# High-half products of a pair of weight pieces first, low-half products last, in a mixture-of-experts stage

## The chip, the core and the metric

The kernel runs on one core of one Trainium2 chip. Its metric is device time in microseconds for one execution. Each run gives one such time; a profiled execution gives a trace beside it.

## The reference, cut to what matters

Two blocks of two layers each run over 256 tokens of width 1024. The change touches only the feed-forward part of the first block's second layer, a mixture of eight experts of which each token uses two:

```
logits = x @ w_router + b_router
top_vals, top_idx = top_k(logits, 2);  top_w = softmax(top_vals)
combine = sum(one_hot(top_idx, 8) * top_w[..., None], axis=-2)
for e in range(8):
    out += combine[..., e:e+1] * ((silu(x @ w_gate[e]) * (x @ w_up[e])) @ w_down[e])
```

`w_gate` and `w_up` are 1024x3584 for each expert and `w_down` is 3584x1024, all in float32.

## The kernel before

**Three products for one.** TensorE multiplies fp32r numbers, which keep fewer bits than float32. Each float32 operand is therefore held as two fp32r tiles: a high half (the value rounded) and a low half (the value less the high half). A product is the sum of three: high activations by high weights, high activations by low weights, low activations by high weights. `Tensor.mm3` issues them in this order for one slice of 128 rows. The activations are the operand that is loaded (LDWEIGHTS), the weights are the one that streams by, 512 columns at a time, into one bank of PSUM.

**How weights come.** The class `Weights` plans every weight of the program in order. A load brings 1 MB (128 x 2048 floats) from memory into one of five raw buffers `RG`, on SyncE's queue. In the experts' stage a load is cut into a pair of pieces of 1024 columns. ScalarE copies each piece into the high tile (`his`, two ACTIVATEs of 128x1024 per pair). VectorE then writes the low tile of the whole pair with one subtraction of 128x2048 (`los`, the case `both`). The three pairs of tiles are a ring: two are in `WH` (high) and `WL` (low), the third is in `MW`, which holds both halves, so rows that name `MW` are a pair of either half. Three counters order it. `P.hi` rises with each piece that ScalarE has copied. `P.lo` rises with each pair that VectorE has finished, and SyncE refills a raw buffer once it has risen. `P.used` rises when TensorE has finished a piece, and ScalarE waits for it before it overwrites that piece (`p.prev`).

**The stage.** For each expert, 128 gathered tokens are the rows, and the 3584 hidden columns are done in 7 steps of 512. The program numbers the 56 steps j, with `todo[j] = (e, n)`. A step on TensorE is, in this order:

1. G: the gate product, two pairs (24 matmuls), the first of them in `MW`.
2. U: the up product, two pairs (24 matmuls), the first in `WH`/`WL`, the second in `MW`.
3. the extras: at n = 3 the gather of the next expert's tokens (32 small matmuls), at n = 4 two transposes for putting tokens back, at n = 1 the scatter of the last expert's result (8 matmuls, the second half of which waits for VectorE's additions).
4. D: the down product of the step before, two pairs (24 matmuls), into two banks.
5. four transposes of the activated hidden block, once VectorE has multiplied it.

ScalarE's queue for step j is: the high halves of U, silu of G, the high halves of D, at n = 3 the gather's modulation (8 small ACTIVATEs and two copies), the high halves of the next G, at n = 0 the copies of the finished expert's result, and the high half of the transposed block. VectorE's queue is: the low halves of U and D, the multiplication, at n = 1 the scatter's additions, the low halves of the next G, then the low half of the gathered tokens (n = 3) or of the result (n = 0), and the low half of the transposed block. Each engine works through its queue in program order.

The lines that the change touches are `up` and `down` inside `pe_moe`. Both wait for `P.lo` of a pair before any product of it. In the rows below, L205 is the matmul helper, L213 the transpose helper, L197 `act` on ScalarE, L167 `tt` on VectorE (`ATR` is the transposed block, `HTR` the gathered tokens, `DER` the result), L171 `ts` and L175 `stt`.

Of the kernel before, what the change touches and what calls it, by code (L numbers as in the profile page):

```python
# [372 lines left out]
def build(nc, w):  # L373
    ctx = ExitStack()
    with ctx:
# [43 lines left out]
        PS = ctx.enter_context(nc.psum_tensor("PS", [128, 8, 512], F32))  # L419
# [19 lines left out]
        def tok(t):  # L439
            return slice(t * 128, (t + 1) * 128)  # L440
# [1493 lines left out]
        EAT = [ATR[:, z * 1024:(z + 1) * 1024].rearrange("p (u k n) -> p u k n", u=2, k=4) for z in range(2)]  # L1934
        HE = [HTR[:, z, :].rearrange("p (u k n) -> p u k n", u=2, k=8) for z in range(2)]
# [7 lines left out]
        def pe_moe(pe, P, s_pe, s_v, s_a):  # L1943
            def gather(e):
                u = e % 2
                pe.wait_ge(s_v, e, "pp")
                for g in range(2):
                    if e:
                        pe.wait_ge(s_a, e - 1, f"gm{g}")
                        if e > 1:  # L1950
                            pe.wait_ge(s_v, e - 2, f"acc1{g}")
                        if g == 0:
                            pe.wait_ge(s_a, e - 1, "pt")
                    for k in range(4):
                        for t in range(2):
                            x = pe.mm(PS[:, 2 + g, k * 128:(k + 1) * 128], X[:, t, (g * 4 + k) * 128:(g * 4 + k + 1) * 128],
                                      PP[:, u, t], t == 0, t == 1)
                    x.then_inc(s_pe, f"ga{g}")

            def put_back(e):  # L1960
                u = e % 2
                pe.wait_ge(s_a, e, "gm0")
                for t in range(2):
                    x = pe.tr(PS[:, 2, tok(t)], PP[:, u, t], IDN)
                x.then_inc(s_pe, "pb")

            def up(parts, b, u):
                for p in parts:
                    pe.wait_ge(P.lo, p.los)
                    for k in range(p.kk):  # L1970
                        kk = p.k0 + k
                        x = pe.mm3(PS[:, b, :], HE[0][:, u, kk, :], HE[1][:, u, kk, :], p.h3[:, k, :], p.l3[:, k, :], kk == 0,
                                   kk == 7)
                    x.then_inc(P.used)

            def scatter(e):
                u = e % 2
                pe.wait_ge(s_a, e, "pt")
                for t in range(2):
                    for h in range(2):  # L1980
                        c = slice(h * 512, (h + 1) * 512)
                        pe.wait_ge(s_v, e, f"de{h}")
                        if t:
                            pe.wait_ge(s_v, e, f"acc0{h}")
                        elif e:
                            pe.wait_ge(s_v, e - 1, f"acc1{h}")
                        pe.mm(PS[:, 2 + h, :], PT[:, u, tok(t)], DE[0][:, c], True, False)
                        pe.mm(PS[:, 2 + h, :], PT[:, u, tok(t)], DE[1][:, c], False, True).then_inc(s_pe, f"sc{t}{h}")

            def down(j):  # L1990
                e, n = todo[j]
                for p in P.of["moe_down", e, n]:
                    pe.wait_ge(P.lo, p.los)
                    pe.wait_ge(s_v, j, "at")
                    if n == 0 and e:
                        for h in range(2):
                            pe.wait_ge(s_v, e - 1, f"de{h}")
                    i = p.k0
                    for h in range(2):
                        c = slice(h * 512, (h + 1) * 512)  # L2000
                        x = pe.mm3(PS[:, h, :], EAT[0][:, j % 2, i, :], EAT[1][:, j % 2, i, :], p.h3[:, 0, c], p.l3[:, 0, c],
                                   n == 0 and i == 0, n == 6 and i == 3)
                    x.then_inc(P.used)

            gather(0)
            put_back(0)
            for j, (e, n) in enumerate(todo):
                u = j % 2
                if n == 0:
                    for g in range(2):  # L2010
                        pe.wait_ge(s_v, e, f"he{g}")
                if j >= 2:
                    pe.wait_ge(s_v, j - 2, "at")
                up(P.of["moe_gate", e, n], 4 + 2 * u, e % 2)
                if j >= 2:
                    pe.wait_ge(s_v, j - 2, "ac")
                up(P.of["moe_up", e, n], 5 + 2 * u, e % 2)
                if n == 3 and e + 1 < NE:
                    gather(e + 1)
                if n == 4 and e + 1 < NE:  # L2020
                    put_back(e + 1)
                if n == 1 and e:
                    scatter(e - 1)
                if j:
                    down(j - 1)
                pe.wait_ge(s_v, j, "ac")
                for i in range(4):
                    x = pe.tr(PS[:, 4 + 2 * u, i * 128:(i + 1) * 128], EAC[:, u, i * 128:(i + 1) * 128], IDN)
                x.then_inc(s_pe, "at")
            down(len(todo) - 1)  # L2030
            scatter(NE - 1)

# [1285 lines left out]
```

## Time and profile before

| what | value |
|---|---|
| median of three runs | 2967.05 us (2965.32 to 2967.56) |
| span of the profiled execution | 2961.7 us |
| TensorE busy (modelled ends) | 2550.9 us, 86% |
| weight loads of TensorE | 2001.1 us, 68% |
| VectorE busy | 2062.3 us, 70% |
| ScalarE busy | 1557.5 us, 53% |
| 16 DMA engines in the experts' stage | 89% |

The span is measured from the first to the last instruction of one profiled execution; no separate time of that execution is listed, so 5.35 us is what lies between its span and the median of the runs. Times in the rows are microseconds from the start of that span. The experts' stage reaches from about 905 to 1988 us. TensorE's matmul ends are modelled, so its waits are read from its weight loads (PEld), each of which stands just before its matmul.

### The profile page before, as it was taken

What the parts mean: (1) busy time and instruction counts of PE and PEld (TensorE: products, weight loads), DVE (VectorE), ACT (ScalarE), POOL (GpSimd) and SP (SyncE); (2) the same over time, 40 slices, a digit from 0 to 9 for tenths busy, and PEclk for the clock granted to TensorE, in tenths of its full rate; (3) what the DMA queues carried; (4) which work ended last, traced back from release to release, by engine and by line L of the source; (5) the groups of instructions that cost most, each with busy time, mean ns of one, the idle gap of its engine ahead of it and who ended that gap; (6) DMA issues with size and microseconds to landing.
All of it is one profiled execution on the core that took longest, in us unless ns stands there. A gap on an engine that the chain in (4) does not pass through costs nothing.

```text
span 2961.7 us, 31514 instructions
## 1 busy us (share of the span) xinstructions
PE 2550.9 (86%) x11727; PEld 2001.1 (68%) x11727; DVE 2062.3 (70%) x2214; ACT 1557.5 (53%) x1920; POOL 24.0 (1%) x33
## 2 busy tenths in 40 slices
PE   6977789977967999999999999976777998886898
PEld 2736677856556777777777777765556786655787
DVE  6687786755666888787878888875665554575454
ACT  1222434442156778787777777764534544544443
POOL 0000000000100000000000000000000000000000
PEclk8997999986978999999999999998877999977899
DMA  7450367732335898898989899984112454303352
GB/s 252 160 164 29 106 214 263 270 120 71 100 114 200 323 332 324 300 361 291 362 302 353 330 333 329 335 295 136 44 43 100 157 185 156 109 15 114 104 188 93
DMA packets 274306, 598.03 MB, mean 202 GB/s; under 512 B 28705, under 2 KB 35167, under 8 KB 272993
## 3 DMA queue, kind: packets, MB, share of 16 engines
q1 hardware_dynamic: 252144, 580.30, 55.2%
q10 hardware_dynamic: 22002, 15.66, 2.0%
q8 instruction: 93, 1.52, 0.2%
q14 instruction: 67, 0.55, 0.1%
HBM read 594.86 MB, written 1.06 MB: 201 GB/s over the span
## 4 chain that ended last, share of the span: by engine, by line
PE 61%; DVE 24%; ACT 10%; issue 2%; ACTq 2%; DMA 1%; DVEq 0%; POOL 0%; POOLq 0%; PEldq 0%
PE PS L205 58%; DVE WL L167 8%; ACT WH L197 3%; ACT AR L197 2%; PE PS L213 2%; DVE MW L167 2%; DVE AR L167 2%; ACTq L146 2%; DVE WF L167 1%; DVE MOD L167 1%; ACT MW L197 1%; ACT L197 1%; DVE HF L167 1%; ACT WF L197 1%; DVE HTR L167 1%
## 5 line engine op out<-in xcount | busy, mean ns | idle before, releaser
L167 DVE TENSOR_TENSOR WL<-RG,WH 128x1024 fp32r<-128x1024 f32 (+1 forms) x558 | 919.4, 1648 | 447.4 <-ACT WH L197 422.8
L197 ACT ACTIVATE WH<-RG 128x1024 fp32r<-128x1024 f32 x782 | 827.3, 1058 | 597.4 <-PE PS L205 527.2
L205 PE MATMUL PS<-WH,HTR 128*128 128x512 f32 (+3 forms) x2920 | 926.0, 393 | 66.8 <-DVE HTR L167 23.4
L205 PEld LDWEIGHTS PS<-WH,HTR 128*128 128x128 f32 x2920 | 558.0, 194 | 201.0 <-DVE WL L167 39.8
L205 PE MATMUL PS<-WL,HTR 128*128 128x512 f32 (+3 forms) x1460 | 568.9, 390 | 0.0
L205 PE MATMUL PS<-WH,ATR 128*128 128x512 f32 x1624 | 523.6, 396 | 16.4 <-DVE WL L167 9.1
L205 PEld LDWEIGHTS PS<-WH,ATR 128*128 128x128 f32 x1624 | 310.3, 191 | 84.7 <-DVE WL L167 18.3
L205 PE MATMUL PS<-MW,HTR 128*128 128x512 f32 x1332 | 331.1, 398 | 18.2 <-DVE MW L167 18.2
L205 PE MATMUL PS<-WL,ATR 128*128 128x512 f32 x812 | 320.4, 395 | 0.0
L205 PEld LDWEIGHTS PS<-WL,HTR 128*128 128x128 f32 x1460 | 283.2, 194 | 52.4
L167 DVE TENSOR_TENSOR MW<-RG,MW 128x2048 fp32r<-128x2048 f32 x112 | 256.7, 2292 | 63.3 <-ACT MW L197 52.6
L205 PEld LDWEIGHTS PS<-MW,HTR 128*128 128x128 f32 x1332 | 249.0, 190 | 70.6 <-DVE MW L167 20.1
L197 ACT ACTIVATE MW<-RG 128x1024 fp32r<-128x1024 f32 x224 | 237.9, 1062 | 24.7 <-PE PS L205 2.1
L205 PEld LDWEIGHTS PS<-WL,ATR 128*128 128x128 f32 x812 | 155.2, 191 | 31.9
L213 PE MATMUL PS<-KC,AR 128*128 128x128 f32 (+2 forms) x716 | 115.8, 300 | 59.5 <-DVE AR L167 34.6
L213 PEld LDWEIGHTS PS<-KC,AR 128*128 128x128 f32 (+2 forms) x716 | 94.6, 155 | 85.7 <-DVE AR L167 41.0
L197 ACT ACTIVATE AR<-PS 128x512 f32<-128x512 f32 (+3 forms) x112 | 63.7, 569 | 107.0 <-PE PS L205 59.1
L197 ACT ACTIVATE AR<-PS,SMALL 128x128 f32<-128x128 f32 (+3 forms) x146 | 77.6, 531 | 73.3 <-PE PS L205 65.4
L197 ACT ACTIVATE ATR<-PS 128x512 fp32r<-128x512 f32 x102 | 61.2, 600 | 80.5 <-PE PS L213 75.5
L205 PE MATMUL PS<-RG,CZ 128*4 128x512 f32 x192 | 92.6, 636 | 10.5 <-DMA RG<-in_mod_w 9.8
L213 PE MATMUL PS<-KC,X 128*128 128x128 f32 x160 | 31.8, 377 | 80.3 <-ACTq L155 30.4
L213 PEld LDWEIGHTS PS<-KC,X 128*128 128x128 f32 x160 | 27.9, 200 | 84.6 <-DVEq L155 36.6
(224 smaller groups left out, 2057.5 us busy)
## 6 DMA issues: line engine op xcount, KB each, us to landing
RG<-in_moe_w_gate SPq DMA_DIRECT2D x112, 1024.0 KB, 5.4
RG<-in_moe_w_up SPq DMA_DIRECT2D x112, 1024.0 KB, 5.8
RG<-in_moe_w_down SPq DMA_DIRECT2D x112, 1024.0 KB, 6.0
RG<-in_w_ff SPq DMA_DIRECT2D x64, 1024.0 KB, 5.2
RG<-in_mod_w SPq DMA_DIRECT2D x48, 1024.0 KB, 5.2
RG<-in_w_in SPq DMA_DIRECT2D x36, 1024.0 KB, 5.2
RG<-in_w_out SPq DMA_DIRECT2D x16, 1024.0 KB, 5.1
RG<-in_ffn_w_gate SPq DMA_DIRECT2D x14, 1024.0 KB, 5.2
```

The lines of the kernel that those rows point to most:

```text
L146: return Ins(self.e.dma_start(dst, src, **kw) if self.e is not None else None, self)
L167: return self.did(lambda: self.e.tensor_tensor(o, a, b, op))
L197: return self.did(lambda: self.e.activation(o, a, f, bias=bias, scale=scale))
L205: return self.did(lambda: self.e.matmul(o, l, r, start=start, stop=stop))
L213: return self.did(lambda: self.e.transpose(o, a, perm))
```

## The change

TensorE takes the two pieces of a pair together. For each piece it waits for ScalarE's high half of that piece and issues the two products that need only high weights (high activations, then low activations). Then it waits for the pair's low half and issues the third product for both pieces, each followed by its `P.used`. In `down` the waits for the activated block and for the last result's tiles stand once, ahead of all pieces. The number of matmuls, their shapes and their banks stay, and so do the queues of all other engines.

```diff
             def up(parts, b, u):
-                for p in parts:
-                    pe.wait_ge(P.lo, p.los)
-                    for k in range(p.kk):
-                        kk = p.k0 + k
-                        x = pe.mm3(PS[:, b, :], HE[0][:, u, kk, :], HE[1][:, u, kk, :], p.h3[:, k, :], p.l3[:, k, :], kk == 0,
-                                   kk == 7)
-                    x.then_inc(P.used)
+                for pair in (parts[0:2], parts[2:4]):
+                    for p in pair:
+                        pe.wait_ge(P.hi, p.i + 1)
+                        for k in range(p.kk):
+                            kk = p.k0 + k
+                            pe.mm(PS[:, b, :], HE[0][:, u, kk, :], p.h3[:, k, :], kk == 0, False)
+                            pe.mm(PS[:, b, :], HE[1][:, u, kk, :], p.h3[:, k, :], False, False)
+                    for p in pair:
+                        pe.wait_ge(P.lo, p.los)
+                        for k in range(p.kk):
+                            kk = p.k0 + k
+                            x = pe.mm(PS[:, b, :], HE[0][:, u, kk, :], p.l3[:, k, :], False, kk == 7)
+                        x.then_inc(P.used)
 
             def down(j):
                 e, n = todo[j]
-                for p in P.of["moe_down", e, n]:
-                    pe.wait_ge(P.lo, p.los)
-                    pe.wait_ge(s_v, j, "at")
-                    if n == 0 and e:
+                parts = P.of["moe_down", e, n]
+                pe.wait_ge(s_v, j, "at")
+                if n == 0 and e:
+                    for h in range(2):
+                        pe.wait_ge(s_v, e - 1, f"de{h}")
+                for pair in (parts[0:2], parts[2:4]):
+                    for p in pair:
+                        pe.wait_ge(P.hi, p.i + 1)
                         for h in range(2):
-                            pe.wait_ge(s_v, e - 1, f"de{h}")
-                    i = p.k0
-                    for h in range(2):
-                        c = slice(h * 512, (h + 1) * 512)
-                        x = pe.mm3(PS[:, h, :], EAT[0][:, j % 2, i, :], EAT[1][:, j % 2, i, :], p.h3[:, 0, c], p.l3[:, 0, c],
-                                   n == 0 and i == 0, n == 6 and i == 3)
-                    x.then_inc(P.used)
+                            c = slice(h * 512, (h + 1) * 512)
+                            pe.mm(PS[:, h, :], EAT[0][:, j % 2, p.k0, :], p.h3[:, 0, c], n == 0 and p.k0 == 0, False)
+                            pe.mm(PS[:, h, :], EAT[1][:, j % 2, p.k0, :], p.h3[:, 0, c], False, False)
+                    for p in pair:
+                        pe.wait_ge(P.lo, p.los)
+                        for h in range(2):
+                            c = slice(h * 512, (h + 1) * 512)
+                            x = pe.mm(PS[:, h, :], EAT[0][:, j % 2, p.k0, :], p.l3[:, 0, c], False, n == 6 and p.k0 == 3)
+                        x.then_inc(P.used)
```

## Rows read from the trace of the kernel before

**Rows 1.** The page's first line.

```profile
span 2961.7 us, 31514 instructions
```

**Rows 2.** Windows of stage and steady steps: busy us (instructions) by engine, clock, DMA share, GB/s.

```profile
905.00:1988.00 1083.00, 1019.30 (x4574) 823.09 (x4572) 897.82 (x528) 830.33 (x886) 0.00 (x0) 0.99 0.89 325
1545.00:1596.00 51.00, 51.00 (x230) 41.51 (x229) 45.26 (x25) 41.85 (x42) 0.00 (x0) 1.00 1.03 379
1566.00:1600.00 34.00, 34.00 (x153) 27.66 (x152) 30.49 (x17) 28.43 (x30) 0.00 (x0) 1.00 1.04 393
```

**Rows 3.** Waits of TensorE's weight loads, 905 to 1978: us, times, longest.

```profile
PEld PS L205 <- DVE WL L167: 40.2, 56, 2.8
PEld PS L205 <- DVE AR L175: 23.2, 14, 3.1
PEld PS L205 <- DVE MW L167: 20.1, 8, 2.6
```

**Rows 4.** Timeline of weight loads: start, us, work, count, [idle before it <- releaser].

```profile
926.94 2.59 PEld L205 LDWEIGHTS PS<-MW,HTR 128*128 128x128 f32 x12 [1.98 <-DVE MW L167]
...
1550.88 0.19 PEld L205 LDWEIGHTS PS<-WH,HTR 128*128 128x128 f32 x1 [0.30 <-DVE WL L167]
...
1567.88 0.19 PEld L205 LDWEIGHTS PS<-WH,HTR 128*128 128x128 f32 x1 [0.30 <-DVE WL L167]
...
1945.55 0.19 PEld L205 LDWEIGHTS PS<-WH,HTR 128*128 128x128 f32 x1 [0.30 <-DVE WL L167]
```

**Rows 5.** Timelines of ScalarE and VectorE, from 1545 us.

```profile
1545.57 0.60 ACT L197 ACTIVATE ATR<-PS 128x512 fp32r<-128x512 f32 x1 [0.89 <-PE PS L213]
1546.28 2.21 ACT L197 ACTIVATE WH<-RG 128x1024 fp32r<-128x1024 f32 x2
...
1548.53 2.29 DVE L167 TENSOR_TENSOR WL<-RG,WH 128x2048 fp32r<-128x2048 f32 x1 [0.66 <-ACT WH L197]
```

**Rows 6.** Timelines of weight loads, ScalarE and VectorE around one gather.

```profile
1523.28 0.58 PEld L213 LDWEIGHTS PS<-KC,AR 128*128 128x128 f32 x4
1526.46 2.61 PEld L205 LDWEIGHTS PS<-MW,HTR 128*128 128x128 f32 x12 [2.59 <-DVE MW L167]
...
1533.64 0.19 PEld L205 LDWEIGHTS PS<-WH,HTR 128*128 128x128 f32 x1 [1.85 <-DVE WL L167]
...
1516.46 3.96 ACT L197 ACTIVATE AR<-PS,SMALL 128x128 f32<-128x128 f32 x8 [2.45 <-PE PS L205]
...
1521.87 2.21 ACT L197 ACTIVATE MW<-RG 128x1024 fp32r<-128x1024 f32 x2
...
1524.11 2.29 DVE L167 TENSOR_TENSOR MW<-RG,MW 128x2048 fp32r<-128x2048 f32 x1 [6.88 <-ACT MW L197]
...
1528.90 1.49 DVE L167 TENSOR_TENSOR HTR<-AR,HTR 128x512 fp32r<-128x512 f32 x2
...
1531.29 2.30 DVE L167 TENSOR_TENSOR WL<-RG,WH 128x2048 fp32r<-128x2048 f32 x1
```

**Rows 7.** Around scatters: two weight-load rows, then three pieces of the chain.

```profile
1062.20 0.19 PEld L205 LDWEIGHTS PS<-WH,HTR 128*128 128x128 f32 x1 [1.47 <-DVE WL L167]
...
1871.55 0.19 PEld L205 LDWEIGHTS PS<-WH,HTR 128*128 128x128 f32 x1 [1.45 <-DVE WL L167]
...
1462.58 0.61 ACT DER L197
...
1479.69 6.19 PE PS L205 x26
...
1207.99 7.81 PE PS L205 x26
```

**Rows 8.** Waits of ScalarE, 905 to 1976: us, times, longest.

```profile
ACT WH L197 <- PE PS L205: 49.6, 31, 6.4
...
ACT MW L197 <- PE PS L205: 2.1, 6, 0.5
ACT WH L197 <- DMA RG<-in_moe_w_gate: 1.6, 2, 1.2
```

## The prediction

> **What bounds the kernel now.** I read the busy time by windows first: it says which engine is close to full in the experts' stage. Then I read TensorE's waits in that stage, and last the timelines of the three engines at each kind of wait, because only there can one see what is late next. All sums are made against the profiled span of 2961.7 us [rows 1]; the median of the runs is 5.35 us more, and I add that at the end.
>
> The stage takes 1083 us, 37% of the span. TensorE's matmuls are shown busy for 1019 us of it, VectorE for 898, ScalarE for 830, the DMA engines for 89% [rows 2]. So TensorE sets the pace, but the others follow closely, and a wait that is removed can come back at another place.
>
> TensorE waits for low halves 64 times, for 40.2 + 20.1 = 60.3 us, and for the scatter's additions 14 times, for 23.2 us [rows 3]. The change can only touch the 60.3 us. A product row of 12 loads takes 2.61 us, so one product of 512 columns costs about 0.22 us [rows 6], and the eight products with high weights of a pair take 8 x 0.22 = 1.8 us. The change lets TensorE run them before the low half is there: each wait shrinks by up to 1.8 us, if the high half is there and if the time is not lost again further on. A gap of some 0.04 us stands before every load anyway, and I take it off each wait.
>
> **The change by places.** I sorted the 64 waits by where they stand.
>
> *Forty-one short waits in ordinary steps.* The first is 1.98 us, the last 0.30 us [rows 4]; most are 0.25 to 0.55 us, and they add up to 19.9 us. The pattern is in one step: ScalarE's copy of the transposed block waits for TensorE's transposes and starts at 1545.57, the high half of U's first pair takes 1546.28 to 1548.49, VectorE's low half 1548.53 to 1550.82 [rows 5], and TensorE starts U at 1550.88 [rows 4]. The high half is there about 2 us before G ends, and the low half will be wanted 1.8 us after U starts, so it is in time with 1.5 us to spare. Nothing else stands behind: a step then takes 17.00 - 0.26 = 16.74 us, while VectorE's own work in a step is six subtractions and two small ones, 6 x 2.4 + 2 x 0.8 = 16.0 us with gaps. Six of the longer ones are 0.9 to 1.2 us (in the first four experts, where VectorE has an operation more between its low halves), so the 1.8 us cover them; the first, 1.98 us, is covered but for 0.1 us. The working: 19.9 - 41 x 0.04 = 18.3 us gained.
>
> *Seven gathers, with two waits each.* Here ScalarE is late: it does the eight modulations from 1516.46 and two copies, and only then the high half of G's first pair, 1521.87 to 1524.08. TensorE is ready at about 1523.9 and waits 2.59 us, until VectorE is through at 1526.40; then it waits 1.85 us more before U, until VectorE's low half of that pair, 1531.29 to 1533.59, is done [rows 6]. After the change it starts G at once, since both high pieces are there in time, and wants G's first low half at 1523.9 + 1.8 = 1525.7, for which it waits 0.7 us. G's two pairs of 2.7 us then end at 1530.0, U's low half is wanted at 1531.8, and that comes no earlier than before: VectorE is busy without a gap from 1524.11 over the tokens' low halves at 1528.90 to 1533.59 [rows 6]. That is the binding event in both kernels. Before, twelve products of the pair follow it; after, four. So the gain is 8 x 0.22 = 1.76 us, not the 4.4 us of the two waits: 7 x 1.75 = 12.3 us. A wait of 1533.6 - 1531.8 = 1.8 us stays inside U's first pair. In three of the seven gathers the second wait is short and the pair before it runs at a lower clock; from the start of G to the start of U it is 7.18 us in each of the seven, so the argument is the same.
>
> *Seven waits just ahead of a scatter.* The first is 1.47 us, the last 1.45 us [rows 7]; together 11.0 us. I count nothing for them. From the copy of the finished expert's result at 1462.58, ScalarE works without a gap (result, transposed block, high halves of U, silu, high halves of D), then VectorE takes over with the low halves of D, the multiplication and the additions, and TensorE goes on at 1479.69 [rows 7]. This path of 17.1 us does not run through TensorE's U. TensorE will reach the scatter 1.5 us earlier and wait there 1.5 us longer: the waits for additions should grow from 23.2 us to about 34 us.
>
> *The end of the stage.* The last wait for a low half (2.8 us, the longest in [rows 3]) also covers the transposed block, which VectorE makes after the low halves; `down` waits for it first in either kernel. It and the 0.30 us ahead of it give nothing.
>
> *What is added.* TensorE has three waits for a pair instead of one, 672 more in 336 pairs. I take them at nothing: while TensorE is busy its waits are met long before, and 51 us of ordinary steps show it busy for 51.00 us with a wait at every second piece [rows 2]. From the other side, if one cost as much as the gap that stands before each load anyway, 0.04 us, they would take 27 us; see the rivals. The first piece of a pair is given back after product 10 instead of 6, 0.9 us later. ScalarE waits for TensorE's pieces 31 times in `WH` [rows 8]. Where it does, the pair's high half is finished 0.65 us later, because the second piece is given back at the same time as before; TensorE has 1.8 us more patience for the low half, so this is hidden. At the other places ScalarE comes later than the release anyway. The moved waits in `down` stand where the first piece's stood, and nothing new is queued behind them.
>
> *The clock.* After a scatter's wait TensorE sometimes runs at 1.2 instead of 2.4 GHz for a while: the same 26 products take 7.81 us after one scatter and 6.19 us after another [rows 7]. This is so in five of the seven. With a wait that is 1.5 us longer I expect it in all seven: 2 x 1.6 = 3 us lost.
>
> Sum: 18.3 + 12.3 - 3.0 = 27.6 us. 2961.7 - 27.6 = 2934.1 us of span, and with the 5.35 us 2939.5; I say 2940 us.
>
> **The rivals.**
>
> *The transfers set the pace (12 in 100).* A step reads six loads of 1.049 MB, 6.29 MB. At 16.74 us a step that is 376 GB/s. Ordinary steps show 379 GB/s over 51 us with a DMA share of 1.03, and 393 GB/s over 34 us [rows 2], the extra being a catch-up; ScalarE waited for a transfer twice, 1.6 us in all [rows 8]. So there are 4% to spare. If they are not usable, because transfers land later when they overlap more, the ordinary steps stay at 17.0 us: some 33 of the short waits, 33 x 0.26 = 8.6 us, come back as waits for ScalarE's high halves. Time: 2948 us. The Trainium skill (HBM Reference, Specifications) puts the effective rate of a core at about 358 GB/s; by it a step could not take less than 17.6 us and the change would bring nothing. This trace disagrees: 393 GB/s here, with one core at work, and I keep the measured rate.
>
> *The clock falls more often (10 in 100).* The clock fell in three of the seven gathers too, where it was hidden behind U's low half. After the change the waits there are 0.7 and 1.8 us instead of 2.6 and 1.9, which speaks against it. If it fell in all seven behind the binding event, it would cost 7 x 1.6 = 11 us: 2951 us. The Trainium skill (TensorE: Matmul & The Clock Gate, Part 1) says the array is slow by default and activity frees it, which agrees with the two durations of 26 products.
>
> *More comes back (7 in 100).* If VectorE's chain behind a gather itself moves forward, the 26.3 us of the two waits are all gained instead of 12.3: 2926 us. Against it stands VectorE without a gap there.
>
> *The added waits cost (5 in 100).* At 0.04 us each, 27 us, they would eat the gain: 2967 us, no change. For it: after a wait a load starts 0.04 us later. Against: nothing is seen at the waits that are already met.
>
> *Slower, by the later release (4 in 100).* At 37 places (31 in `WH`, six in `MW`) ScalarE stands waiting for TensorE [rows 8]. If there the loop ScalarE, VectorE, TensorE is closed, each costs up to 0.9 us, 33 us; it decides from 0.82 us a place on (30.6 / 37), where it equals the gain. With the clock's 3 us it makes 2973 us. Against it: the low half may now be 1.8 us late at no cost, twice the delay.
>
> **How the numbers follow.** The forecast has 62 in 100. The range of 2928 to 2956 us takes in the transfers and the clock and reaches almost to the greater gain; that one, the added waits and the slower case are left out, 16 in 100, and some 4 in 100 for mixtures beyond it. What a measurement of this kernel can tell from no change is 0.2%, 6 us. Faster by more than that: 62 + 12 + 10 + 7 = 91 in 100, less one for a mixture of the losses: 90. Within 0.2%: 5. Slower: 5.
>
> **What would show it.** In the trace after: waits for low halves fall from 60 us to about 20 us (seven of 1.8 and seven of 0.7 us after gathers, 2.8 at the end), now standing at loads of the last four products; waits for additions rise to about 34 us; ordinary steps take 16.7 us instead of 17.0; an expert takes about 3.2 us less, the first four somewhat more; the stages before 905 us and after the last expert are unchanged. Waits for high halves longer than 0.1 us in ordinary steps would mean that transfers or releases bind, and small gaps at the start of each piece that the added waits cost.

## The result, and the profile after

The changed kernel takes 2946.05 us (median of four runs, 2943.81 to 2952.73) against 2967.31 us. The ratio of the runs is 0.9933, with a 95% interval of 0.9921 to 0.9945: 16 to 23 us faster. I had forecast 2940 us. The run with the profile took 2947.36 us. Its page begins as follows (the first two lines, and the chain by line):

```profile
span 2945.6 us, 31514 instructions
...
PE 2539.9 (86%) x11727; PEld 2008.4 (68%) x11727; DVE 2062.1 (70%) x2214; ACT 1557.1 (53%) x1920; POOL 23.9 (1%) x33
...
PE PS L205 62%; DVE WL L167 6%; PE PS L213 3%; ACT AR L197 2%; DVE MW L167 2%; DVE AR L167 2%; ACTq L146 2%; DVE WF L167 1%; DVE MOD L167 1%; ACT WH L197 1%; DVE HF L167 1%; ACT L197 1%; DVE HTR L167 1%; ACT WF L197 1%; DVE SMALL L178 1%
```

The same work is done, and the other engines are as busy as before. In this execution the experts' stage begins 4.3 us later than in the one of before (its first four transposes load at 928.87 us against 924.54 us), for reasons ahead of the change. So I compare the stage by itself, from those transposes to the last ones of the 56 steps: 1048.84 us before, 1029.27 us after, 19.6 us less.

The waits of TensorE's weight loads from 905 to 1978 us (us, times, longest), to be held against [rows 3]:

```profile
PEld PS L205 <- DVE AR L175: 34.3, 16, 4.5
PEld PS L205 <- DVE WL L167: 15.5, 10, 2.0
PEld PS L205 <- DVE MW L167: 6.8, 8, 0.9
```

The waits for low halves fell from 60.3 us in 64 places to 22.3 us in 18. The last of the 64, 2.8 us at the stage's end, is not among the 18: it is now put down to the transposed block, with 3.0 us. The stage now ends earlier, so this window takes in two waits for additions at its end that the window of [rows 3] leaves out. Without these two the waits for the scatter's additions are 33.2 us in 14 places: they rose by 10.0 us from 23.2.

The timeline of one gather, first the weight loads, then VectorE (start, us, work, count, idle before). It answers to [rows 6]:

```profile
1511.98 0.58 PEld L213 LDWEIGHTS PS<-KC,AR 128*128 128x128 f32 x4
1512.53 1.69 PEld L205 LDWEIGHTS PS<-MW,HTR 128*128 128x128 f32 x8
1515.14 0.76 PEld L205 LDWEIGHTS PS<-MW,HTR 128*128 128x128 f32 x4 [0.92 <-DVE MW L167]
1515.95 1.78 PEld L205 LDWEIGHTS PS<-WH,HTR 128*128 128x128 f32 x8
1517.77 0.87 PEld L205 LDWEIGHTS PS<-WL,HTR 128*128 128x128 f32 x4
1518.68 1.77 PEld L205 LDWEIGHTS PS<-WH,HTR 128*128 128x128 f32 x8
1522.32 0.76 PEld L205 LDWEIGHTS PS<-WL,HTR 128*128 128x128 f32 x4 [1.87 <-DVE WL L167]
...
1512.80 2.29 DVE L167 TENSOR_TENSOR MW<-RG,MW 128x2048 fp32r<-128x2048 f32 x1 [6.48 <-ACT MW L197]
1515.19 2.29 DVE L167 TENSOR_TENSOR WL<-RG,WH 128x2048 fp32r<-128x2048 f32 x1
1517.59 1.49 DVE L167 TENSOR_TENSOR HTR<-AR,HTR 128x512 fp32r<-128x512 f32 x2
1519.18 0.69 DVE L167 TENSOR_TENSOR ATR<-PS,ATR 128x512 fp32r<-128x512 f32 x1
1519.98 2.29 DVE L167 TENSOR_TENSOR WL<-RG,WH 128x2048 fp32r<-128x2048 f32 x1
```

Here one sees the change: eight loads, then four. After the transposes TensorE starts G's first pair at once. It waits 0.92 us for the first low half, goes through G's second pair, and waits 1.87 us inside U's first pair. VectorE has no gap from 1512.80 on, and its low half of that pair ends at 1522.27.

The timeline of the weight loads at one scatter, to be held against [rows 7]:

```profile
1457.55 2.68 PEld L205 LDWEIGHTS PS<-MW,HTR 128*128 128x128 f32 x12
1460.27 0.87 PEld L205 LDWEIGHTS PS<-DER,PTR 128*128 128x128 f32 x4
1465.69 0.50 PEld L205 LDWEIGHTS PS<-DER,PTR 128*128 128x128 f32 x2 [4.55 <-DVE AR L175]
1466.54 0.50 PEld L205 LDWEIGHTS PS<-DER,PTR 128*128 128x128 f32 x2 [0.35 <-DVE AR L175]
1467.14 3.32 PEld L205 LDWEIGHTS PS<-WH,ATR 128*128 128x128 f32 x8
1470.55 1.49 PEld L205 LDWEIGHTS PS<-WL,ATR 128*128 128x128 f32 x4
1472.08 1.77 PEld L205 LDWEIGHTS PS<-WH,ATR 128*128 128x128 f32 x8
1473.90 0.87 PEld L205 LDWEIGHTS PS<-WL,ATR 128*128 128x128 f32 x4
```

No low half is waited for, and TensorE is at the scatter early; then it stands for 4.55 us. Behind that wait eight loads take 3.32 us, and 1.77 us five microseconds later: the clock has fallen. The windows of the granted clock behind this scatter, and one behind the same scatter in the kernel before, which is one of the two of its seven behind which the clock had not fallen (busy us of PE, PEld, DVE, ACT, POOL with counts, granted clock, DMA share, GB/s):

```profile
1466.50:1469.90 3.40, 3.40 (x9) 2.68 (x9) 2.74 (x3) 0.00 (x0) 0.00 (x0) 0.50 0.75 297
1469.90:1473.30 3.40, 3.40 (x12) 2.68 (x12) 1.05 (x1) 1.16 (x2) 0.00 (x0) 0.71 0.39 76
1473.30:1476.70 3.40, 3.40 (x19) 2.82 (x18) 2.30 (x2) 1.88 (x3) 0.00 (x0) 1.00 0.57 235
```

```profile
1479.70:1483.10 3.40, 3.40 (x15) 2.83 (x16) 3.15 (x3) 1.06 (x1) 0.00 (x0) 1.00 0.63 251
```

After: 0.50 (1.2 GHz), then 0.71 in a window that holds both levels, then 1.00. Before, with a wait of 3.08 us: 1.00 (2.4 GHz).

The 56 sets of transposes bound 55 steps, each from one set to the next. Taking them apart shows where the 19.6 us come from (sums in us):

| steps | before | after | difference |
|---|---|---|---|
| seven behind a gather | 149.9 | 137.2 | -12.8 |
| seven with a scatter | 169.2 | 178.3 | +9.1 |
| the other 41 | 729.7 | 713.9 | -15.9 |

An ordinary step went from 17.00 to 16.80 us. A step with a scatter went from 23.2 to 24.9 us to 24.1 to 26.8 us.

### The profile page after: what moved, and what is told of

The parts are those of the page before. It is cut to its first block, busy times and chain, and to the rows that moved or that the text cites. A ratio compares the mean times of both kernels' runs of the same rounds, so it can differ in the third digit from the quotient of the medians.

```text
span 2945.6 us, 31514 instructions
## 1 busy us (share of the span) xinstructions
PE 2539.9 (86%) x11727; PEld 2008.4 (68%) x11727; DVE 2062.1 (70%) x2214; ACT 1557.1 (53%) x1920; POOL 23.9 (1%) x33
## 4 chain that ended last, share of the span: by engine, by line
PE 65%; DVE 22%; ACT 7%; issue 2%; ACTq 2%; DMA 2%; DVEq 0%; POOL 0%; POOLq 0%; PEldq 0%
PE PS L205 62%; DVE WL L167 6%; PE PS L213 3%; ACT AR L197 2%; DVE MW L167 2%; DVE AR L167 2%; ACTq L146 2%; DVE WF L167 1%; DVE MOD L167 1%; ACT WH L197 1%; DVE HF L167 1%; ACT L197 1%; DVE HTR L167 1%; ACT WF L197 1%; DVE SMALL L178 1%
## 5 line engine op out<-in xcount | busy, mean ns | idle before, releaser
L205 PE MATMUL PS<-WH,HTR 128*128 128x512 f32 (+3 forms) x2920 | 850.4, 391 | 47.5 <-DVE HTR L167 23.4
L205 PE MATMUL PS<-WL,HTR 128*128 128x512 f32 (+3 forms) x1460 | 513.9, 390 | 11.6 <-DVE WL L167 11.6
L205 PE MATMUL PS<-WH,ATR 128*128 128x512 f32 x1624 | 465.4, 400 | 16.2 <-DVE WL L167 8.9
L205 PE MATMUL PS<-WL,ATR 128*128 128x512 f32 x812 | 265.3, 393 | 0.0
L197 ACT ACTIVATE MW<-RG 128x1024 fp32r<-128x1024 f32 x224 | 237.9, 1062 | 24.2 <-DMA RG<-in_moe_w_gate 1.5
```

The costliest lines, as they stand in the source:

```text
L197: return self.did(lambda: self.e.activation(o, a, f, bias=bias, scale=scale))
L205: return self.did(lambda: self.e.matmul(o, l, r, start=start, stop=stop))
```

## The experiments

Twelve kernels ran, in three rounds of four and each round on another chip, always beside the kernel before (2966.2, 2968.3 and 2968.1 us). The times in this table are medians in us. The ratio is to the kernel before on the same chip, so it is the better measure between rounds.

| run | edit | us | ratio (95%) |
|---|---|---|---|
| after_again | none | 2945.0 | 0.9926 (0.9905 to 0.9947) |
| up_only | new order in gate and up alone | 2952.0 | 0.9958 (0.9945 to 0.9971) |
| down_only | new order in down alone | 2965.4 | 0.9989 (0.9980 to 0.9997) |
| after_busy | changed kernel, products in the scatter's wait | 2934.0 | 0.9895 (0.9875 to 0.9914) |
| before_busy | kernel before, products in the scatter's wait | 2960.6 | 0.9977 (0.9966 to 0.9989) |
| up_busy | gate and up alone, products in the wait | 2945.6 | 0.9927 (0.9915 to 0.9939) |
| piecewise | low half waited for in each piece | 2952.2 | 0.9953 (0.9940 to 0.9966) |
| more_waits | 2016 waits added that are already met | 2947.6 | 0.9925 (0.9912 to 0.9939) |
| rows_moved | two rows loaded at a gather | 2945.2 | 0.9923 (0.9910 to 0.9937) |
| split_scatter | changed kernel, scatter's second half behind down | 2916.4 | 0.9819 (0.9803 to 0.9835) |
| before_split | kernel before, the same split | 2975.4 | 1.0023 (1.0012 to 1.0033) |
| split_rows | split_scatter and rows_moved | 2912.6 | 0.9821 (0.9806 to 0.9837) |

**The changed kernel again.**

> The changed kernel once more, beside the others on the same chip. Both theories: some 2946 us, 0.993 of the kernel before. The theory that the clock takes back a part of the gain expects the seven steps with a scatter to be 9 us longer in sum than before again (between 6 and 12, since the clock's falls vary), and every other step to be shorter.

It took 2945.0 us, and its seven scatter steps are again the long ones, 24.1 to 26.1 us. The granted clock fell behind each.

**Is it the clock? Products in the wait.** The scatter gets N products that nobody reads, between its two halves. N is 17 in the changed kernel, 10 in the kernel before, 15 with gate and up alone:

```diff
                 for t in range(2):
+                    if t and j is not None:
+                        pe.wait_ge(s_v, j - 1, "at")
+                        for i in range(N):
+                            pe.mm(PS[:, 6 - 2 * (j % 2), :], PT[:, u, tok(0)], DE[0][:, 0:512], True, True)
                     for h in range(2):
```

> The changed kernel with 17 products of 512 columns more in each of the seven scatters, between its two halves, where TensorE otherwise waits 4.2 to 4.5 us for VectorE's additions; they write a bank that nobody reads afterwards, so nothing else is computed. Theory (the clock falls during that wait and TensorE runs slowly behind it): the granted clock stays at 1.00 in all seven, the steps with a scatter shrink from some 25.5 us to some 23 us, and the kernel takes 2946 - 14 = 2932 us, at least under 2938 us. Rival (those steps are longer for another reason, as a late transfer or a late high half): no gain, 2946 us or some more.

> The kernel before with 10 such products in the same place, where it waits 2.7 to 3.1 us. Theory: five of its seven scatters ran slowly behind the wait, 1.5 us each, so it gains 7 us: 2960 us. Beside the run with the 17 products it then shows the change without the clock: 28 us apart. Rival: 2967 us, and 21 us apart.

Both came out as the theory said: 2934.0 and 2960.6 us. The timeline and a window of the changed kernel with the products:

```profile
1454.62 4.72 PEld L205 LDWEIGHTS PS<-DER,PTR 128*128 128x128 f32 x21
1460.04 0.30 PEld L205 LDWEIGHTS PS<-DER,PTR 128*128 128x128 f32 x2 [0.70 <-DVE AR L175]
1460.90 0.30 PEld L205 LDWEIGHTS PS<-DER,PTR 128*128 128x128 f32 x2 [0.56 <-DVE AR L175]
1461.24 1.80 PEld L205 LDWEIGHTS PS<-WH,ATR 128*128 128x128 f32 x8
```

```profile
1440.00:1475.00 35.00, 34.60 (x156) 28.03 (x155) 30.23 (x21) 24.28 (x27) 0.00 (x0) 1.00 0.90 311
```

TensorE waits as long for the additions, since it only fills the time, and it comes back at full clock: the eight loads take 1.80 us instead of 3.32. Work that computes nothing gains 11 us on the changed kernel and 5.6 us on the one before. Taken apart by steps, the scatter steps are 163.4 us with the products against 178.3 without, and in the kernel before 161.8 against 169.2. So the clock's falls cost 14.8 us after and 7.4 us before. All other steps together are unchanged within 0.1 us.

**Which part gives the gain?**

> Only the gate and up products take the new order, the down products keep the old one. Theory (no wait for a low half that mattered stood ahead of a down product): the same time as the changed kernel within 3 us, 2946 us. Rival (the new order in the down products gives a part of the gain, since their pairs come right behind VectorE's low halves): half of the gain is missing, 2955 us.

> Only the down products take the new order, gate and up keep the old one. In the kernel before no wait for a low half stood at a down pair except the last; with gate and up alone changed, waits of 0.24 and 0.88 us appeared there. Theory (the new order of the down pairs only covers waits that the earlier arrival brings): no gain by itself, 2967 us within 3 us. Rival (its own part is what the run with gate and up alone lacked, 7 us): 2960 us.

> Gate and up in the new order, down in the old, with 15 products more in each scatter to hold the clock. Theory (without the clock's falls the down part of the change is worth 10 us, since the step with gate and up alone waits 0.24 us at an ordinary down pair and 0.88 us behind a gather): 2944 us, 10 us above the changed kernel with its 17 products and 16 below the kernel before with its 10. Rival (the down part is worth 6 us as without the extra products): 2940 us.

The theory for the first was wrong: gate and up alone take 2952.0 us, 7 us more than the whole change. Weight loads of that kernel behind a gather:

```profile
1526.21 0.77 PEld L205 LDWEIGHTS PS<-WL,HTR 128*128 128x128 f32 x4 [1.87 <-DVE WL L167]
...
1531.01 0.19 PEld L205 LDWEIGHTS PS<-WH,ATR 128*128 128x128 f32 x1 [0.88 <-DVE WL L167]
```

TensorE, now early, meets the next pair's low half too soon: 0.88 us here, and 0.24 us at the down pair of each ordinary step, which takes 16.91 us instead of 16.80. In the kernel before, no down pair waited, save the last. Down alone takes 2965.4 us, 2.7 us less than before with an interval that ends at 0.9997, so by itself it is worth next to nothing. With the clock held, the down part on top of gate and up is worth 2945.6 - 2934.0 = 11.6 us. These two ran on different chips, but the stages of their traces, 1026.1 and 1014.4 us, differ by as much. I had expected 10. The new order in gate and up uncovers waits that the new order in down must then cover.

**How far ahead must TensorE be able to go?** Here each piece waits for its own low half, after four products instead of eight, and is released as early as before:

```diff
-                for pair in (parts[0:2], parts[2:4]):
-                    for p in pair:
+                for p in parts:
                         pe.wait_ge(P.hi, p.i + 1)
...
-                    for p in pair:
-                        pe.wait_ge(P.lo, p.los)
+                    pe.wait_ge(P.lo, p.los)
```

> Each piece by itself: wait for its high half, four products with high weights, wait for the pair's low half, two products, release. TensorE can then go only 4 x 0.22 = 0.9 us ahead of a low half instead of 1.8 us, and each piece is released as early as in the kernel before. Theory (what counts is how many products stand ahead of the wait for the low half): seven gathers lose 0.9 us each and the ordinary waits of 0.3 us stay covered, but the waits of 1 to 1.2 us show again: some 8 us slower than the changed kernel without the clock's part; with longer steps ahead of the scatters its waits there are shorter, so 2950 us, between 2946 and 2956. Rival (the early release matters): 2940 us or less.

2952.2 us, as the theory had it. Weight loads behind the same gather:

```profile
1516.75 1.69 PEld L205 LDWEIGHTS PS<-MW,HTR 128*128 128x128 f32 x8 [1.85 <-DVE MW L167]
...
1523.93 0.30 PEld L205 LDWEIGHTS PS<-WL,HTR 128*128 128x128 f32 x2 [1.87 <-DVE WL L167]
```

The first wait is 0.93 us longer than the 0.92 us of the changed kernel: four products. A step behind a gather takes 20.5 us instead of 19.6, and the steps of the first experts in which VectorE has an operation more take 17.1 to 17.3 us instead of 16.79. Ordinary steps stay at 16.80 us: four products ahead are enough for their wait of 0.3 us. The early release of the first piece brought nothing that could be seen.

**Do the added waits cost?** Three waits are repeated behind each wait for a low half, that is six for a pair:

```diff
                         pe.wait_ge(P.lo, p.los)
+                        pe.again(P.lo, p.los)
+                        pe.again(P.lo, p.los)
+                        pe.again(P.lo, p.los)
```

> The changed kernel with six more waits for each pair on TensorE (three behind each wait for the low half), all of them already met when they are reached. Theory (a wait that is met is hidden behind the matmuls under way): 2946 us, ordinary steps stay at 16.80 us. Rival (each costs 0.04 us): six pairs a step, 36 waits, 1.4 us a step, 56 steps: 80 us slower.

2947.6 us, and the ordinary steps take 16.79 or 16.80 us as before. The stage took 1029.59 us against 1029.27. The steps behind a gather are 0.2 us longer each: their first wait for a low half is 1.10 us instead of 0.92, so repeated waits right behind a true wait do show. In ordinary steps three times as many added waits as the change brings cost nothing that can be seen.

**Late transfers?** The two rows of the next normalisation are loaded elsewhere:

```diff
-a_ln_rows(a, 1, "ffn", 2) if (e, n) == (4, 5) else None
+a_ln_rows(a, 1, "ffn", 2) if (e, n) == (5, 3) else None
```

> The changed kernel with ScalarE's loading of the two rows for the next normalisation (1 MB) moved from the ordinary step 5 of the fifth expert to step 3 of the sixth, a gather, where the transfers pause. Theory (the fifth expert's scatter step is 1.3 us longer than the others since high halves wait for late transfers there): the wait of 2.0 us ahead of that scatter goes, 1 to 2 us gained, within what can be measured: 2945 us; ScalarE waits some 5 us less for transfers. Rival (the transfers are late in every ordinary step): as many waits for transfers as before, spread over the experts.

2945.2 us: nothing that can be measured. The fifth expert's scatter step went from 26.8 to 25.9 us, and the wait of 2.04 us for a low half in it to 0.22. ScalarE's waits for transfers went from 10.2 us (changed kernel, below: us, times, longest, 905 to 1976 us) to 6.9 us in 13 places. That fall can't be put down to the edit: the same waits sum to 11.0 us in the second run of the changed kernel and to 3.9 us in the one with the added waits.

```profile
ACT WH L197 <- DMA RG<-in_moe_w_gate: 6.5, 9, 1.6
ACT WH L197 <- DMA RG<-in_moe_w_down: 2.0, 2, 1.6
ACT MW L197 <- DMA RG<-in_moe_w_gate: 1.5, 4, 0.5
ACT MW L197 <- DMA RG<-in_moe_w_up: 0.2, 1, 0.2
```

In the kernel before it was 1.6 us [rows 8]. So transfers have come closer to the pace. In this trace ordinary steps take 16.80 us with or without these waits: ScalarE's late high halves stay covered. They do so barely: in the second run of the changed kernel two steps of the fifth expert, with waits of up to 1.35 us for transfers, took 16.95 and 17.01 us.

**A version that beats both.** The second half of each scatter goes behind the down product:

```diff
                 if n == 1 and e:
-                    scatter(e - 1)
+                    scatter(e - 1, (0,))
                 if j:
                     down(j - 1)
+                if n == 1 and e:
+                    scatter(e - 1, (1,))
```

> The changed kernel with the second half of each scatter moved behind the down product of the same step, so that VectorE's additions run while TensorE multiplies. Theory (TensorE's wait of 4.2 us ahead of the scatter's second half and the clock's fall behind it are all of that place): both go, a step with a scatter takes 19 to 21 us instead of 25.5 us and the next ones lose under 1 us of it: 7 x 5 = 35 us less, 2910 us, between 2900 and 2925, and the granted clock stays at 1.00. Rival (ScalarE's and VectorE's chain from the last result to the additions sets the pace anyway, and the wait comes back at the next pair): 2938 us, the clock's part alone.

> The changed kernel with the split scatter and the two rows loaded at the sixth expert's gather instead of the fifth's step 5. Theory: the fifth expert's wait of 1.1 us ahead of its scatter and most of ScalarE's 10 us of waits for transfers go; 1 us of time, so 2915 us within 3 us, no measurable difference to the split alone (2916 us). Rival (transfers bound the ordinary steps of the split version): 2908 us or less.

> The kernel before with the second half of each scatter moved behind the down product, the order of the products left as it was. Theory: the wait of 2.7 to 3.1 us and the clock's falls go, but VectorE's additions come 1 us later and TensorE is again held by the next low halves: a scatter step from 24.2 to some 20 us, 7 x 4 = 28 us less, half a microsecond of it lost in each next step: 2942 us, between 2935 and 2950. If the two changes simply added up, the split would give here what it gave on the changed kernel, 29 us: 2938 us.

On the changed kernel the split brings it to 2916.4 us, within what was expected, and 2912.6 us with the rows moved, which is not told apart from it. Weight loads of the split kernel at a scatter:

```profile
1448.52 0.87 PEld L205 LDWEIGHTS PS<-DER,PTR 128*128 128x128 f32 x4
1449.43 1.77 PEld L205 LDWEIGHTS PS<-WH,ATR 128*128 128x128 f32 x8
...
1454.87 0.87 PEld L205 LDWEIGHTS PS<-DER,PTR 128*128 128x128 f32 x4
1455.77 0.58 PEld L213 LDWEIGHTS PS<-KC,AR 128*128 128x128 f32 x4
...
1459.80 0.77 PEld L205 LDWEIGHTS PS<-MW,HTR 128*128 128x128 f32 x4 [1.78 <-DVE MW L167]
```

There is no wait inside the scatter, and the granted clock stays at 1.00 behind all seven. What comes back is 1.78 us ahead of the next low half. Scatter step and next step take 18.6 + 18.6 us instead of 25.5 + 16.8.

On the kernel before, I was far off: I expected 2942 us, and it took 2975.4, slower than before by 0.12 to 0.33%. Weight loads, then VectorE, at one scatter of that kernel:

```profile
1070.43 0.87 PEld L205 LDWEIGHTS PS<-DER,PTR 128*128 128x128 f32 x4
...
1076.78 0.87 PEld L205 LDWEIGHTS PS<-DER,PTR 128*128 128x128 f32 x4
1077.69 0.59 PEld L213 LDWEIGHTS PS<-KC,AR 128*128 128x128 f32 x4
1081.71 3.97 PEld L205 LDWEIGHTS PS<-MW,HTR 128*128 128x128 f32 x12 [3.44 <-DVE MW L167]
...
1073.24 1.62 DVE L175 SCALAR_TENSOR_TENSOR AR<-PS,SMALL,AR 128x512 f32<-128x512 f32 x2
1077.66 1.60 DVE L175 SCALAR_TENSOR_TENSOR AR<-PS,SMALL,AR 128x512 f32<-128x512 f32 x2 [2.80 <-PE PS L205]
1079.36 2.29 DVE L167 TENSOR_TENSOR MW<-RG,MW 128x2048 fp32r<-128x2048 f32 x1
```

VectorE stands 2.80 us for the second half of the scatter, and only then makes the next low half. TensorE came to that half 1.9 us after VectorE's first additions had ended, against 0.1 us in the split kernel with the change; 1.46 us of this is its wait at U, which the change removes. TensorE, which needs that low half before any product of the pair, stands 3.44 us, and the twelve loads behind it take 3.97 instead of 2.6 us: the wait and the clock's fall have only moved. This scatter step shrinks from 24.4 to 20.0 us, and the next grows from 17.0 to 21.7 us. Five of the seven next steps grow so; the two behind which the clock did not fall grow to 20.4 us. The stage of the profiled execution is 3.0 us longer than before, and the medians are 7 us apart; the trace doesn't show where the rest of this lies. The same edit gains 29 us on one kernel and loses 7 us on the other.

## Why the prediction was right, and where it was off

*What bounds the kernel.* Right in the main: the waits for low halves were on the path, and their total was the right ceiling. About 20 us were to be left, with the 2.8 us at the end among them. Counted so, 25.3 us are left: 19.4 at the gathers (17.5 forecast), 3.0 at the end, 0.6 in the first step, where the wait of 1.98 us left 0.33 and not 0.1, and 2.3 ahead of two scatters, where nothing was forecast.

*Forty-one short waits, 18.3 us.* The place and the cover were right, the size a little large: the other 41 steps gained 15.9 us, and that includes a 42nd short wait, just ahead of the last, of which nothing was expected and 0.2 us came. An ordinary step gained 0.20 us, not 0.26. I had taken off 0.04 us for the gap before a load. But in the kernel before, the next load starts 0.11 us after the one that waited (1550.88 and 1550.98 us), where loads otherwise start 0.23 us apart. So 0.12 of the 0.26 us came back at once, and I had not counted that. The other 0.06 us of the gain is spread thinly over the step; no run shows why.

*Seven gathers, 12.3 us.* Right: 12.8 us, 1.82 us each. Both waits that were to be left (0.7 and 1.8 us) were found, at 0.92 and 1.87 us, and the binding event is VectorE's low half of U's first pair. The run with each piece by itself confirmed it from the other side: half as many products ahead, 0.9 us less gained.

*Seven waits ahead of a scatter, nothing.* Right, and this was the largest trap in the table of waits: 11.0 us of waits went, and the waits for additions rose by 10.0 us, with 2.3 us of new waits for low halves ahead of two of the scatters.

*The clock, -3 us.* Right in kind, too small. I had priced two more falls at the cost of those in the rows. The runs with the products show 14.8 us against 7.4 us before: the clock falls in all seven, and behind four of them it stays low for 6.8 us instead of 3.4 us. That the wait grows from 3 to 4.5 us was in the forecast, but not that the low time could double. This is the term that was most wrong: 7.4 us instead of 3. The doubling does not follow from the wait's length alone: with gate and up alone changed, waits of 4.1 to 4.5 us were followed by 3.4 us of low clock in all seven places. The remaining 1.6 us in the scatter steps lie with the clock held too, 1.0 of them in the fifth expert's (24.2 us against 23.2). The rival of more falls behind gathers did not happen: three of seven before, none after.

*Added waits, release, transfers.* The added waits cost nothing that can be seen in ordinary steps, as forecast. The later release was not seen. The rival that transfers set the pace did not happen: an ordinary step went to 16.80 us, which is 374 GB/s by its 6.29 MB. But ScalarE's waits for transfers rose from 1.6 to 10.2 us, which is closer than I had thought. The figure of about 358 GB/s for a core (Trainium skill, HBM Reference, Specifications) was no bound here, and I had read it wrongly. The same section gives it as the share of a core when both cores of a pair stream, and says that a core alone measures well above it. This trace agrees as far as it goes, with 374 GB/s and one core at work.

The sum by the measured terms is 15.9 + 12.8 - 9.1 = 19.6 us, against 27.6 forecast and 21.3 between the medians. The 8 us that are missing are about 4.4 at the clock, 2.4 at the short waits and 1.6 elsewhere in the scatter steps, less 0.5 at the gathers. With the clock held in both kernels the change is worth 2960.6 - 2934.0 = 26.6 us. What stays open is why the clock's low time behind a scatter is sometimes 3.4 and sometimes 6.8 us long in the same program; the runs do not tell.

## What to carry to other kernels

A wait that is removed is worth only what the next binding event allows: look for the engine without a gap behind it, and count the work that still follows that event. Let products that need only what is ready go first across as large a group as the buffers allow; the length of that run is the patience that the kernel has, and it must be there at every pair, not only where waits are seen now. When TensorE becomes early for something that it must wait for anyway, the longer wait can cost the clock as well. Move independent work into it, but test such a move on the kernel that will use it, since it gained 29 us on one and lost 7 us on the other.

## What the runs showed of the hardware

Waits of 2.6 to 3.1 us on TensorE (kernel before) were followed by a granted clock of 0.50 in five of seven places; the other two were the shortest wait, 2.64 us, and the longest, 3.08 us. Waits of 3.5 to 3.9 us (each piece by itself) and of 4.1 to 4.5 us (gate and up alone) were followed by it in all seven, for 3.4 us each. Waits of 4.2 to 4.55 us in the changed kernel were so in all seven too, and in four of these for 6.8 us. Filling the wait with products that nobody reads kept the clock at 1.00 behind all seven scatters, and gained 11 us. And 2016 added waits on TensorE that were already met when it reached them, six for each twelve matmuls, could not be seen in the ordinary steps at all (16.79 to 16.80 us). Right behind a true wait they could: 0.2 us in each step behind a gather.
